# A two-layer diffusion trunk on one core: the normed activations of the MLP kept in a buffer of their own, matmuls on a tile of ones behind the norms' sums, and the last layer's modulation rows left out

## The reference, cut to what matters

```
for l in range(2):
    mod = (silu(cond) @ w_ada[l] + b_ada[l])           # six rows of 1024: shift, scale, gate, twice
    h = rmsnorm(x, norm_mix_w[l]) * (1 + sc_a) + sh_a
    x = x + gt_a * mixer(h)                            # four branches, gated merge, w_out
    h = rmsnorm(x, norm_mlp_w[l]) * (1 + sc_m) + sh_m
    x = x + gt_m * (square(relu(h @ mlp_w1[l])) @ mlp_w2[l])
y = rmsnorm(x, final_norm_w)
```

## Time and profile before

| | |
|---|---|
| time, median of 3 runs (range) | 2731.73 us (2729.89 to 2735.34) |
| the profiled execution | 2735.46 us, span of the core 2733.7 us |
| mean granted TensorE clock | 0.986 of full speed |
| PE busy | 2592.0 us, 95% of the span |
| DVE, ACT, POOL busy | 51%, 36%, 24% |
| DMA | 93 GB/s mean |

### The profile page before, as it was taken

One profiled execution on the slowest core, in us unless ns is written; L12 is line 12 of the kernel. 1 busy time (PEld: TensorE's weight loads), 2 busy tenths in 40 slices (PEclk: granted clock), 3 DMA queues, 4 the chain that ended last, 5 costly groups with the idle time before them and its releaser, 6 DMA issues.

```text
span 2733.7 us, 55262 instructions
## 1 busy us (share of the span) xinstructions
PE 2592.0 (95%) x23844; PEld 2409.0 (88%) x23844; DVE 1392.2 (51%) x2307; ACT 981.5 (36%) x1590; POOL 669.4 (24%) x525
## 2 busy tenths in 40 slices
PE   5998999999999899999989989999999997999998
PEld 5887897889899799999978888788898997999997
DVE  5767624236533746255475775342454338255364
ACT  4251043334422544253342501433344226253352
POOL 2322122222233220211222311222232331211202
PEclk9999999999999999999999999999999999999999
DMA  8110012433343223223330100134232422232222
GB/s 344 39 55 3 3 59 89 139 106 103 107 141 116 70 80 114 87 92 107 123 138 25 47 4 12 59 133 138 91 111 100 150 98 73 83 101 99 95 93 85
DMA packets 75453, 253.79 MB, mean 93 GB/s; under 512 B 8084, under 2 KB 20532, under 8 KB 74192
## 3 DMA queue, kind: packets, MB, share of 16 engines
q1 hardware_dynamic: 72240, 226.60, 24.7%
q0 software_dynamic: 2976, 23.69, 2.3%
HBM read 233.05 MB, written 17.20 MB: 92 GB/s over the span
## 4 chain that ended last, share of the span: by engine, by line
PE 83%; DVE 8%; ACT 4%; issue 2%; DMA 1%; POOL 0%; SPq 0%; DVEq 0%; ACTq 0%; POOLq 0%
PE ps_dense L1028 29%; PE ps_dense L1036 17%; PE ps_dense L1886 6%; PE ps_aux L1028 4%; PE ps_dense L1653 3%; PE ps_dense L1890 3%; PE ps_aux L1417 2%; PE ps_dense L1731 1%; PE ps_aux L1653 1%; PE ps_aux L1707 1%; PE ps_dense L1062 1%; PE ps_aux L1403 1%; PE ps_dense L1719 1%; PE ps_aux L1369 1%; DMA arena<-in_w_early 1%
## 5 line engine op out<-in xcount | busy, mean ns | idle before, releaser
L858 POOL TENSOR_TENSOR w_low<-w_ring,w_high 128x256 fp32r<-128x256 f32 (+1 forms) x338 | 518.5, 1552 | 1465.7 <-ACT w_high L2040 1459.4
L2040 ACT ACTIVATE w_high<-w_ring 128x1024 fp32r<-128x1024 f32 x200 | 212.0, 1060 | 460.1 <-PE ps_dense L1028 263.6
L1028 PE MATMUL ps_dense<-z_both,w_high 128*128 128x320 f32 x2048 | 313.6, 310 | 0.0
L1028 PEld LDWEIGHTS ps_dense<-z_both,w_high 128*128 128x128 f32 x2048 | 302.1, 188 | 3.7 <-issue 3.2
L1036 PE MATMUL ps_dense<-h_high,w_high 128*128 128x320 f32 x1024 | 242.2, 318 | 7.1 <-DVE x_res L3030 3.1
L1028 PE MATMUL ps_dense<-h_high,w_high 128*128 128x320 f32 x864 | 209.3, 325 | 32.9 <-ACT h_high L2080 30.1
L1036 PE MATMUL ps_dense<-h_high,w_low 128*128 128x320 f32 x1024 | 233.2, 309 | 0.0
L1036 PE MATMUL ps_dense<-h_low,w_high 128*128 128x320 f32 x1024 | 232.5, 308 | 0.0
L3174 DVE SCALAR_TENSOR_TENSOR x_res<-ps_dense,mod,x_res 128x320 f32<-128x320 f32 (+2 forms) x192 | 72.6, 433 | 298.0 <-PE ps_dense L1028 298.0
L1028 PEld LDWEIGHTS ps_dense<-h_high,w_high 128*128 128x128 f32 x864 | 151.1, 198 | 44.9 <-issue 36.7
L1028 PE MATMUL ps_dense<-h_low,w_high 128*128 128x320 f32 x864 | 188.2, 310 | 0.0
(11 more groups left out here) (523 smaller groups left out, 5092.8 us busy)
## 6 DMA issues: line engine op xcount, KB each, us to landing
w_ring<-in_w_mlp SPq DMA_DIRECT2D x128, 512.0 KB, 3.6
w_ring<-in_w_gate SPq DMA_DIRECT2D x64, 640.0 KB, 4.0
w_ring<-in_w_late SPq DMA_DIRECT2D x64, 512.0 KB, 4.9
w_ring<-in_w_in SPq DMA_DIRECT2D x48, 512.0 KB, 3.5
w_ring<-in_w_early SPq DMA_DIRECT2D x32, 512.0 KB, 3.5
w_ring<-in_w_out SPq DMA_DIRECT2D x16, 512.0 KB, 3.4
arena<-in_dft POOLq DMA_DIRECT2D x2, 2944.0 KB, 14.5
x_kept<-x_res POOLq DMA_DIRECT2D x2, 2560.0 KB, 11.9
```

The source lines that it names most:

```text
L858: last = g.tensor_tensor(w_low[:, n % 2, k:k + step], ring[:, slot, k:k + step, :], w_high[:, n % 2, k:k + step].bitcast(F32), ALU.subtract)
L1028: last = mm(out[:, s, 0:HALF], w_[:, par_, k, :], x_[:, k, s * HALF:(s + 1) * HALF], start=first, stop=final)
L2040: a(w_high[:, n % 2], ring[:, j, 0:KC, :], ACT.Copy).then_inc(w_high_in.sem, 1)
```

## The change

It has three parts. (1) The MLP's norm writes its result into `bout` (seen as `h_kept`, the same shape as `h`) and no longer into `h_norm`. `h_kept` isn't overwritten by squares, so `quadrant_totals` makes each T from it by one subtraction, each into a quadrant that isn't needed any more; ACT's wait ahead of its first two `total_high` is for the third difference and no longer the fourth. (2) Behind `norm_sum` PE makes 31 products of the tile of ones with itself, 128 columns each, into a free PSUM bank (`stay_busy`), in the MLP norm of both layers and behind the first layer's MLP. (3) In the last layer `w_early` isn't loaded, multiplied, copied or turned; its places in the ring's count are counted by the neighbours (`places`, `then_inc` of 2 or 3), and SP adds to `ring_in` by an empty instruction behind the same wait.

```diff
+        h_kept = bout.rearrange("p b c t -> p (b c) t")
+        SUM_AT = {1: (0, 0), 2: (1, 1), 3: (0, 1), 4: (1, 0)}
         def t_sum(i):
-            return of_quadrant(bout.rearrange("p b c t -> p (b c) t"), i - 1)
+            return b_quadrant(h_kept, *SUM_AT[i])
         def t_low(i):
-            return of_quadrant(bout_low.rearrange("p b c t -> p (b c) t"), i - 1)
+            return b_quadrant(bout_low.rearrange("p b c t -> p (b c) t"), *SUM_AT[i])
...
-                        if q % 4 == 1:
+                        if q % 4 == 1 and l + 1 == DEPTH:
+                            sp.wait_ge(block_done.sem, l * N_BLOCKS + g * N_GROUP + (N_EARLY + early_at(q // 4) + 1))
+                            sp.nop().then_inc(ring_in[early_at(q // 4) % RING].sem, 16)
+                        elif q % 4 == 1:
                             load(l, early_at(q // 4), ins["w_early"], ...)
...
+            def stay_busy():
+                for _ in range(31):
+                    mm(psA[:, 2, 0:P], c_("ones"), c_("ones"), start=True, stop=True)
...
                 def early(j):
+                    if l + 1 == DEPTH:
+                        return
...
-                    if j == PACK - 1:
+                    if j == PACK - 1 and l + 1 < DEPTH:
                         turn_rows(l, psA[:, 0, bass.ds(g * (2 * PACK), 2 * PACK)], N_LATE, PACK, g)
...
                 norm_sum(l, 0)
+                stay_busy()
                 mlp(l)
                 pe.wait_ge(*residual.nth(l, 39))
                 norm_sum(l, 1)
+                if l + 1 < DEPTH:
+                    stay_busy()
...
             def modulate(l, which):
+                normed = h_kept if which else h
...
                         if j == 1:
-                            act.wait_ge(*h_last.nth(l, 2 * KC + 4))
+                            act.wait_ge(*h_last.nth(l, 2 * KC + 3))
                             for i in T_ORDER[0:2]:
                                 total_high(i)
                         if j == 3:
+                            act.wait_ge(*h_last.nth(l, 2 * KC + 4))
                             total_high(3)
...
                 dve.wait_ge(*h_split.nth(l, 2 * KC))
-                restore(0, 0, 0)
-                link(restore(1, 0, 1))
-                total(1, restored(1), restored(0))
-                dve.wait_ge(*h_last.nth(l, 2 * KC + 1))
-                link(restore(0, 1, 1))
-                total(3, restored(0), restored(1))
-                total(2, restored(0), t_sum(1))
-                dve.wait_ge(*h_last.nth(l, 2 * KC + 2))
-                link(restore(1, 1, 0))
-                total(4, restored(1), t_sum(2), 3)
+                b11, b12, b21, b22 = (b_quadrant(h_kept, r, c) for r in range(2) for c in range(2))
+                total(1, b12, b11, 0)
+                total(3, b22, b12, 1)
+                total(2, b22, t_sum(1), 2)
+                total(4, b21, t_sum(2), 3)
...
-                    if m == 5:
+                    if m == 5 and l + 1 < DEPTH:
                         keep_early(PACK - 1)
```

More of the change, by code:

```diff
@@ L143 @@
 ROUND = 12582912.0
-DVE_LINKS = 198
+DVE_LINKS = 195
 ACT_LINKS = 23
@@ L635, in raw_quadrant @@
             return quad4(ring[:, j, k:k + 4, :])
-        def of_quadrant(flat, q):
-            return flat.rearrange("p c t -> p (c t)").rearrange("p (k n) -> p k n", n=HALF)[:, 4 * q:4 * q + 4]
+        h_kept = bout.rearrange("p b c t -> p (b c) t")
+        SUM_AT = {1: (0, 0), 2: (1, 1), 3: (0, 1), 4: (1, 0)}
         def t_sum(i):
-            return of_quadrant(bout.rearrange("p b c t -> p (b c) t"), i - 1)
+            return b_quadrant(h_kept, *SUM_AT[i])
         def t_low(i):
-            return of_quadrant(bout_low.rearrange("p b c t -> p (b c) t"), i - 1)
-        def restored(i):
-            return par[:, at_t + i * 4 * HALF:at_t + (i + 1) * 4 * HALF].rearrange("p (k n) -> p k n", n=HALF)
+            return b_quadrant(bout_low.rearrange("p b c t -> p (b c) t"), *SUM_AT[i])
         def t_high(i):
@@ L1039, in split_tile, with dense_split @@
                 return last
-            def dense_split(out, par_, x_high, x_low, low_ready, ready=None):
+            def dense_split(out, par_, x_high, x_low, low_ready, ready=None, places=1):
                 for k in range(KC):
@@ L1050, in dense_split @@
                     last = split_part(out, par_, k, w_low, x_high, False, k == KC - 1)
-                last.then_inc(block_done.sem, 1)
+                last.then_inc(block_done.sem, places)
             def landed(l, place, turns=0):
@@ L1116, in first_blocks @@
                         last = split_part(dense_banks(b), b, k, w_high, h_low, False, k == KC - 1)
-                    last.then_inc(block_done.sem, 1)
+                    last.then_inc(block_done.sem, 2 if which and b and l + 1 == DEPTH else 1)
             def win_block(l, n):
@@ L1962, in mlp_group @@
                     dense_split(dense_banks(m % 2), m % 2, z_high, z_low, block_low(l, g, KC + m),
-                                (lambda k: hid_ready.nth(l, g * KC + k + 1)) if m == 0 else None)
+                                (lambda k: hid_ready.nth(l, g * KC + k + 1)) if m == 0 else None,
+                                2 if m % 4 == 1 and l + 1 == DEPTH else 1)
                     if m % 4 == 1:
@@ L2069, in modulate, with high_of_h @@
                 act.wait_ge(*mod_ready.nth(l, 1 + which))
+                normed = h_kept if which else h
                 for c in range(KC):
                     act.wait_ge(*x_scaled.nth(l, which * KC + c + 1))
-                    chain.link(a(h[:, c, 0:LAT], h[:, c, 0:LAT], ACT.Identity, scale=mod_a[:, which, c, 0:1],
+                    chain.link(a(normed[:, c, 0:LAT], normed[:, c, 0:LAT], ACT.Identity, scale=mod_a[:, which, c, 0:1],
                                  bias=mod[:, which * 24 + c, 0:1]))
-                    high_of_h(l, which * KC + c, c)
+                    high_of_h(l, which * KC + c, c, normed)
                     if which == 0 and c == 0:
                         win_high(l, 1)
-            def high_of_h(l, n, c):
+            def high_of_h(l, n, c, normed):
                 act.wait_ge(*h_last.nth(l, n + 1))
-                a(h_high[:, c], h[:, c], ACT.Copy).then_inc(h_high_in.sem, 1)
+                a(h_high[:, c], normed[:, c], ACT.Copy).then_inc(h_high_in.sem, 1)
             def hyena(l):
@@ L2563, in norm @@
                     return
+                normed = h_kept if which else h
                 for c in range(KC + 1):
                     if c < KC and not ahead:
-                        v.tensor_tensor(h[:, c], x[:, c], rs[:], ALU.mult).then_inc(x_scaled.sem, 1)
+                        v.tensor_tensor(normed[:, c], x[:, c], rs[:], ALU.mult).then_inc(x_scaled.sem, 1)
                     if c:
                         dve.wait_ge(*x_scaled.nth(l, which * KC + c))
-                        v.tensor_scalar(h[:, c - 1, LAT:T], h[:, c - 1, LAT:T], mod_a[:, which, c - 1, 1:2],
+                        v.tensor_scalar(normed[:, c - 1, LAT:T], normed[:, c - 1, LAT:T], mod_a[:, which, c - 1, 1:2],
                                         mod[:, which * 24 + c - 1, 1:2], ALU.mult, ALU.add).then_inc(h_last.sem, 1)
                 for c in range(KC):
-                    low_of_h(l, which * KC + c, c)
+                    low_of_h(l, which * KC + c, c, normed)
             def scale_all():
@@ L2577, in scale_all, with low_of_h @@
                     v.tensor_tensor(h[:, c], x[:, c], rs[:], ALU.mult).then_inc(x_scaled.sem, 1)
-            def low_of_h(l, n, c):
+            def low_of_h(l, n, c, normed):
                 dve.wait_ge(*h_high_in.nth(l, n + 1))
-                v.tensor_tensor(h_low[:, c], h[:, c], h_high[:, c].bitcast(F32), ALU.subtract)\
+                v.tensor_tensor(h_low[:, c], normed[:, c], h_high[:, c].bitcast(F32), ALU.subtract)\
                     .then_inc(h_split.sem, 1)
@@ L3234, in quadrant_totals, with total @@
             def quadrant_totals(l):
-                def total(i, a_, b_, after=None):
-                    if after:
-                        dve.wait_ge(*h_last.nth(l, 2 * KC + after))
+                def total(i, a_, b_, after):
+                    dve.wait_ge(*h_last.nth(l, 2 * KC + after))
                     v.tensor_tensor(t_sum(i), a_, b_, ALU.subtract).then_inc(h_last.sem, 1)
-                def restore(to, r, c):
-                    return v.tensor_tensor(restored(to), b_quadrant(h_high, r, c).bitcast(F32),
-                                           b_quadrant(h_low, r, c).bitcast(F32), ALU.add)
                 dve.wait_ge(*h_split.nth(l, 2 * KC))
-                restore(0, 0, 0)
-                link(restore(1, 0, 1))
-                total(1, restored(1), restored(0))
-                dve.wait_ge(*h_last.nth(l, 2 * KC + 1))
-                link(restore(0, 1, 1))
-                total(3, restored(0), restored(1))
-                total(2, restored(0), t_sum(1))
-                dve.wait_ge(*h_last.nth(l, 2 * KC + 2))
```

(6 more changed lines are left out.)

## The result

The changed kernel takes 2717.01 us (median of 4 executions, 2714.22 to 2719.9), beside 2733.23 us for the kernel before: a ratio of 0.9934, 95% interval 0.9917 to 0.995. That is 16.2 us by the medians, where 15.9 were forecast. A second comparison, further down, gave 0.9942 (0.9928 to 0.9957). The profiled execution took 2714.22 us, with a span of 2712.4. Of all executions in this document one, with part 3 alone, stands apart (4874.08 us): its kernel's ratio leaves it out, and the median of the other 11 is 2727.13 us.

The account below looks back on a forecast made before the run. PE held 83% of the chain, but DVE's and ACT's chain held it around pair 2. 9.2 (4.6 per layer) + 1.7 + 5.0 = 15.9 us off 2731.7 gave 2716; main case 2711 to 2721, wider range 2707 to 2723.

Parts of the forecast that it names:

- forecast 4.6 per layer: MLP norm to pair 3: halved DVE token sums bring product 5 of pair 3 4.6 us sooner per layer, 9.2 in all.
- the allowance for block 3 and for engines that wait for each other in turn: Ahead of T3's rounding: block 3's end and mutual waits cut the 5.3 us gain to 4.6 to 4.8.
- The collision with POOL: MLP norm: low parts of totals meet POOL's `w_low` and start at 944.0 instead of 949.3, 5.3 us sooner.
- forecast 1.7 behind the first MLP: Norm behind the first MLP: products of ones hold full clock, so PE's 56 matmuls end 1.7 us sooner.
- from below 0: Lower bound of the gain behind the first MLP: 0 if the sparse matmuls up to 1389.5 don't hold the clock.
- The 0.4 us in each MLP norm: MLP norms: with products of ones the high products end at 932.4 instead of 932.8, 0.4 us sooner.
- forecast 5.0: Last layer's second halves: eight early rows at 0.57 us and four turns at 0.12 dropped, 5.0 us saved.
- The early rows in the pairs: Last layer's pairs: dropping these rows saves 0, since PE waits for DVE's additions anyway; upper end 1.7 for pair 0.
- B: Behind pair 2 PE is the bound, not the chain: up to 4.6 us more per layer, 2707; chance 0.12.
- C: Low parts collide twice with POOL and the clock falls all the same: gain 9.8 us, 2722; chance 0.15.
- D: Block 3 and its conversion held pair 2 anyway, so only 5.0 us is gained, 2726.7; chance 0.06.
- E: Products of ones don't overlap, 0.288 us per record: 21.8 us lost in the norms, 2737.6; chance 0.05.

Follow-up runs that it names:

- A second comparison: The changed kernel measured again, unaltered, as the base for three further runs: 2717.47 us against 2734.02 for the kernel before, ratio 0.9942.
- part 3 alone: Kernel before with only the last layer's modulation rows removed: 2727.41 us, ratio 0.9971 to the kernel before.
- the ones in pair 2: Changed kernel plus three products of ones ahead of pair 2's early rows and four behind them: 2718.02 us, ratio 0.9948 to the kernel before.
- part 1 alone: Kernel before with only the token sums taken straight from the kept activations: 2725.48 us against 2735.64, ratio 0.996.
- the A22 kernel: Changed kernel with A22's low part made by DVE right behind S2's, ahead of total 3's low part: 2713.11 us, 4.4 us under the changed kernel.
- two more steps: Changed kernel with two unused DVE subtractions of 1.5 us each ahead of the four totals: 2723.73 us, 6.3 us over the changed kernel.
- 90 records: Changed kernel with 45 products of ones instead of 31 behind the first MLP: 2714.16 us, ratio 0.9918 to the kernel before.

## Why the prediction was right

- **Part 1 (forecast 4.6 per layer, measured 5.3).** The mechanism was the forecast one: eight steps become four, ACT's rounding is next, a low part meets POOL's work, and A22's low part carries the rest to the load, S1 and product 5 of pair 3 (5.46 and 5.33 sooner). That this chain decides is shown by the ones in pair 2 and by part 1 alone, where PE had its clock and S1 to product 5 still took 11.98 and 11.99 us, and by the A22 kernel, which shortened it. It doesn't decide alone: PE at the slow clock ended with it in the changed kernel, which the forecast didn't foresee. The size was 0.7 short, and the term at fault is the allowance for block 3 and for engines that wait for each other in turn (5.3 cut to 4.6). ACT waited for neither: between 940 and 956 its one wait is 3.5 us for DVE's weight difference, and T3's rounding came 5.5 us sooner. The collision with POOL was right in sum and wrong in form. Against the norm's sums the low parts started 31.2 us on and not 32.6, the first was then held 1.1 us (2.56 for 1.48), and the weight difference behind them came 5.5 us sooner where 5.3 were forecast.
- **Slack.** After the result I had read DVE's new idle times as room that the totals could fill. They can't: two more steps cost 2.6 us of 3.0.
- **Part 2 (forecast 1.7 behind the first MLP, measured 0).** The term was mis-sized from its first factor: 0.145 us a record, from a row whose operands change, against 0.11. The products ended 1.9 us sooner than worked out, and the clock fell in the gap. The bound "from below 0" was for another reason (sparse matmuls), but it is the case that came. With 90 records the clock held and the stage fell by 0.8 on average, 1.4 against the trace of before, so the mechanism was right, the filling too short, and the term too large: the stage of before (23.78) was the longest of the three without records. The 0.4 us in each MLP norm is borne out by part 1 with the ones and without (0.3 and, with a less certain pair, 0.9).
- **Part 3 (forecast 5.0, measured 7.0 in the second halves).** The step took the rows' own time from the trace and left out what the stream loses at its breaks, 0.5 us per half. The early rows in the pairs saved nothing that shows, as said: the first halves lie within their scatter with the rows and without.
- **The sum.** 10.6 for the two norm stages, 0 and 7.0 are 17.6 us, less some 0.5 that the rest of the first MLP takes back (389.65 on average in the kernels with the new totals, 389.2 in the three without; the loads' landings differ there, and the cause wasn't tested). That leaves 17 against 15.9 forecast and 16.2 and 16.6 measured by medians. Two terms were too small and one too large: that the total lies 0.3 us off is partly luck.
- **The rivals.** B (PE is the bound) was false for this change: it needs the load sooner, and where it is, the stage is 68.2 us, 2.3 per layer under the changed kernel, not 4.6. C was right in one of its steps (the clock falls all the same) and wrong in the other. D is excluded by the 5.0 and 4.4 us of part 1 alone. E is excluded by 0.11 us a record. Of the forecast's signs, the granted clock of 1.0 came in two of the three norms.

The prediction weighed a sentence of the Trainium skill, "Advanced Engine Details and Errata", section "GPSIMD Details": POOL and DVE conflict on instructions with two SBUF inputs. The runs agree: the four totals took 6.07 us clear of POOL and 8.16 beside it.

## What to carry to other kernels

When steps are taken off an engine's chain, ask what the freed time runs into. Here half of 10 us was left because ACT's rounding, POOL's `w_low` and then a load were next, and moving the one DVE step that frees a load's slot gained 2.3 us more per layer. Work that only keeps PE busy must last until the next engine is really ahead of it, so take its price from a row with the same operands or measure it. And an edit worth 1 to 5 us is read by cutting the traces at the same rows, since the stages it doesn't touch scatter by more.

## What was not expected of the hardware

- A product of ones (128x128 stationary, 128 columns, fp32) is two records of 0.11 us back to back (62 in 7.09 us, 90 in 10.21), where 64 records of the same shape with changing operands stand at 0.145.
- The clock can fall when PE is already at work again. In the second layer's pair 2 of the changed kernel PE stood for 2.35 us, and the windows of 2 us show 1.00 while it stood and 0.50 after it had resumed:

```profile
2294.00:2296.00 2.00, 0.21 (x2) 0.00 (x0) 2.00 (x5) 0.00 (x0) 0.00 (x0) 1.00 0.00 0
2296.00:2298.00 2.00, 1.44 (x9) 1.47 (x10) 0.95 (x3) 0.00 (x0) 0.00 (x0) 0.93 0.88 309
2298.00:2300.00 2.00, 2.00 (x9) 2.00 (x8) 1.25 (x2) 1.19 (x2) 0.00 (x0) 0.50 0.94 299
```

- In the first layer's pair 2 it fell after two waits of 0.69 and 0.96 us with 0.65 us of narrow matmuls between them. The same two waits (0.71 and 0.95 us with part 1 alone, 0.70 and 0.95 with two more DVE steps) left it at 1.00, and so did one wait of 1.12 us behind the same narrow matmuls (the A22 kernel). So the waits alone don't decide it; what does stays open.
- Breaking a stream of full matmuls for the rows costs, beside their own time, about 0.17 us at a break (0.5 us over three).
